# Inverting the pair triangles by 32x32 diagonal blocks in a hybrid DeltaNet and attention decoder step

## What is computed

```python
decay = jnp.where(incl, jnp.exp(jnp.where(incl, diff, 0.0)), 0.0)
L = jnp.where(strict, jnp.einsum('bhnid,bhnjd->bhnij', kb, k) * decay, 0.0)
rhs = jnp.concatenate([vb, kb * jnp.exp(G)[..., None]], axis=-1)
sol = lax.linalg.triangular_solve(L, rhs, left_side=True, lower=True, unit_diagonal=True)
```

## Time and profile before

| | before |
|---|---|
| median of 3 executions (lowest to highest) | 1484.63 us (1483.99 to 1484.95) |
| the profiled execution's own time | 1484.91 us |
| its span in the trace | 1483.1 us |
| TensorE matmuls busy | 1473.2 us (99%), 9284 records |
| VectorE busy | 813.6 us (55%) |
| ScalarE busy | 878.8 us (59%) |
| mean granted TensorE clock | 0.998 |
| DMA | 173.92 MB, mean 117 GB/s |

### The profile page before, as it was taken

The page is one execution under the profiler, slowest core; times in us unless marked ns, Lnnn a source line. Parts: engine busy times, 40 slices in busy tenths (PEclk is TensorE's granted clock), DMA queues, the critical chain, the costliest instruction groups (busy, mean ns, idle before and its releaser), DMA issues.

```text
span 1483.1 us, 26962 instructions
## 1 busy us (share of the span) xinstructions
PE 1473.2 (99%) x9284; PEld 1221.0 (82%) x9284; DVE 813.6 (55%) x1596; ACT 878.8 (59%) x2836; POOL 216.0 (15%) x111
## 2 busy tenths in 40 slices
PE   9999999999999999999999999999999999999998
PEld 7877777877877778778777777788777999999998
DVE  5864445555445563555554555645423766787643
ACT  5545678686566675576855666765766353444432
POOL 3001111211121111111221111111313000000000
PEclk9999999999999999999999999999999999999999
DMA  9542315643245443255323464322654465555551
GB/s 286 169 116 36 78 31 129 153 96 63 61 98 128 119 91 71 61 128 135 83 61 68 102 153 73 68 62 64 169 100 128 151 222 196 171 171 171 190 178 58
DMA packets 263714, 173.92 MB, mean 117 GB/s; under 512 B 165464, under 2 KB 212088, under 8 KB 263448
## 3 DMA queue, kind: packets, MB, share of 16 engines
q1 hardware_dynamic: 263266, 171.94, 44.5%
q10 hardware_dynamic: 318, 0.33, 0.1%
HBM read 132.63 MB, written 6.74 MB: 94 GB/s over the span
## 4 chain that ended last, share of the span: by engine, by line
PE 97%; DVE 2%; ACT 1%; issue 0%; POOL 0%; DVEq 0%; ACTq 0%
PE ps L1991 17%; PE ps L1993 16%; PE ps L1992 16%; PE ps L2400 6%; PE ps L2401 6%; PE ps L2402 5%; PE ps L2031 2%; PE ps L2012 2%; PE ps L2084 2%; PE ps L2348 2%; PE ps L2349 2%; PE ps L2085 2%; PE ps L2086 2%; PE ps L2350 2%; PE ps L1869 2%; PE ps L2150 2%
## 5 line engine op out<-in xcount | busy, mean ns | idle before, releaser
L846 ACT ACTIVATE ksq<-ps 128x128 f32<-128x128 f32 x1024 | 268.1, 276 | 295.0 <-PE ps L1993 293.7
L1991 PE MATMUL ps<-ukh,cTh 128*128 128x512 f32 x1024 | 417.9, 408 | 0.3 <-DVE cTl L1233 0.3
L1993 PE MATMUL ps<-ukh,cTl 128*128 128x512 f32 x1024 | 401.7, 392 | 0.0
L1992 PE MATMUL ps<-ukl,cTh 128*128 128x512 f32 x1024 | 400.4, 391 | 0.0
L700 POOL TENSOR_TENSOR rk<-kss,mhalf 128x32 f32<-128x32 f32 x32 | 179.7, 5616 | 496.8 <-DVE kss L1659 496.8
L1991 PEld LDWEIGHTS ps<-ukh,cTh 128*128 128x128 f32 x1024 | 192.8, 188 | 53.8 <-issue 17.1
L1993 PEld LDWEIGHTS ps<-ukh,cTl 128*128 128x128 f32 x1024 | 192.3, 188 | 42.6
L1992 PEld LDWEIGHTS ps<-ukl,cTh 128*128 128x128 f32 x1024 | 193.2, 189 | 34.1
L846 ACT ACTIVATION_READ_ACCUMULATOR ksq<-ps 128x1 f32 x1024 | 212.2, 207 | 0.0
L834 ACT ACTIVATE cTr<-turned 128x1024 uint16<-128x1024 uint16 x126 | 173.9, 1380 | 10.9 <-PE ps L2015 6.7
L1035 ACT ACTIVATE wh<-wraw 128x2048 fp32r<-128x2048 f32 x44 | 84.3, 1916 | 131.7 <-PE ps L2402 127.2
(11 more groups left out here) (501 smaller groups left out, 2692.4 us busy)
## 6 DMA issues: line engine op xcount, KB each, us to landing
clat<-cache_mla SPq DMA_DIRECT2D x128, 256.0 KB, 2.6
wraw<-w_in SPq DMA_DIRECT2D x16, 1024.0 KB, 5.1
wraw<-w_up SPq DMA_DIRECT2D x16, 1024.0 KB, 5.3
wraw<-w_down SPq DMA_DIRECT2D x16, 1024.0 KB, 5.0
braw<-w_in SPq DMA_DIRECT2D x24, 512.0 KB, 4.1
crope<-cache_mla SPq DMA_DIRECT2D x128, 32.0 KB, 2.4
sst<-state_gdn SPq DMA_DIRECT2D x32, 128.0 KB, 3.3
gdn_sample<-sst SPq DMA_DIRECT2D x32, 128.0 KB, 2.0
```

The costliest lines, as they stand in the source:

```text
L846: i = nc.scalar.activation(ksq[:, P * h:P * h + P], ps[:, k % 3, P * h:P * h + P], ACT.Square, accum_out=kss[:, n // 4 % 2, n % 4, 4 * hal ...
L1991: mm(out, cTh[:, n % 2, c], ukh[:, c, cols], start=c == 0, stop=False)
L1992: mm(out, cTh[:, n % 2, c], ukl[:, c, cols], start=False, stop=False)
L1993: i = mm(out, cTl[:, n % 2, c], ukh[:, c, cols], start=False, stop=c == 3)
```

## The change

The diagonal blocks of 32x32 are inverted apart, in compact tiles Tc, Uc and Xc of 128x(4x32): partition block q holds the q-th diagonal block of each of the four triangles. Levels 1 to 4 are products of 32x32x32, one for each block and triangle (16 for x, 16 for t), each on its own rows and columns of the array. VectorE makes the transpose Uc from Tc itself, by an instruction that turns each 32x32 block (5 for each pair), instead of TensorE (L2141, L2154) and ScalarE (L957). At k = 30 VectorE spreads Tc and Uc into T_ (now 128x(4x64)) and U_ (zeroed first). Level 5 is done on blocks of 32 (8 products at k = 30, 12 at k = 31) and level 6 on blocks of 64 (4 products at k = 32, 4 at k = 33). The masks of the constants shrink from 128 to 32 columns (`consts` loses 800 columns, 410 KB of one DMA). The cut places are marked by "...".

```diff
--- before.py
+++ after.py
@@ -62,14 +62,15 @@
 C_ID, C_BD, C_ROT, C_ONE = _col(P), _col(P), _col(P), _col(P)
 C_COS, C_SIN = _col(T), _col(T)
 C_INCL, C_STRICT = _col(P), _col(P)
-C_LVL = [_col(P) for _ in range(LEVELS)]
+C_LVL = [_col(32) for _ in range(5)]
 C_NEG = _col(3 * P)
 C_ZW = _col(48)
 C_ZP = _col(16)
 C_RSC = _col(1)
 C_RIN = _col(1)
 C_RSQ = _col(1)
-C_LVT = _col(P)
+C_LVT = _col(32)
+C_IDC = _col(32)
 C_THIRDS = _col(16)
 C_HEADS = _col(8)
 C_ALL = _at
@@ -90,19 +91,20 @@
     c[:, C_SIN] = np.tile(np.sin(ang).T, (4, 1))
     c[:, C_INCL] = k <= m
     c[:, C_STRICT] = k < m
+    r, m32 = k % 32, np.arange(32)[None, :]
     for s, at in enumerate(C_LVL):
         b = 1 << s
-        c[:, at] = (k // (2 * b) == m // (2 * b)) & (k % (2 * b) >= b) & (m % (2 * b) < b)
+        c[:, at] = (r // (2 * b) == m32 // (2 * b)) & (r % (2 * b) >= b) & (m32 % (2 * b) < b)
     neg = np.where(m > k, np.float32(-1e30), np.float32(0.0))
     c[:, C_NEG] = np.concatenate([neg, np.zeros((P, P)), neg], 1)
     c[:, C_ZW.start + 15] = 1
     c[0:64, C_ZP.start + 6] = c[64:128, C_ZP.start + 7] = 1
...
-    c[:, C_LVT] = c[:, C_LVL[0]].T
+    c[:, C_LVT] = (r == m32 - 1) & (r % 2 == 0)
+    c[:, C_IDC] = r == m32
     c[:, C_HEADS] = k % 32 == m[:, 0:8]
     c[0:96, C_THIRDS] = k[0:96] % 32 == m[:, 0:16]
     return c
@@ -134,11 +136,11 @@
 F_END = F_ATT + H + 3
 STEPS = list(range(14)) + [None, 14, 15, 16, None] + list(range(17, 47))
 B_START, B_SLOTS = F_END + 6, len(STEPS)
-PAIR_A = ([f"p{j}" for j in range(6)] + ["gr0", "gr1", "l2r", "br0", "br1", "lb0", "lb1", "lb2", "lb3", "qk", "kk", "qks", "kqs", "x0", "kqsT", "x1", "t1"])
+PAIR_A = ([f"p{j}" for j in range(6)] + ["gr0", "gr1", "l2r", "br0", "br1", "lb0", "lb1", "lb2", "lb3", "qk", "kk", "qks", "kqs", "kqsT", "x1", "t1"])
 for _s in range(2, LEVELS):
     PAIR_A += [f"x{_s}", f"t{_s}" if _s < LEVELS - 1 else f"u{_s}"]
 PAIR_A += ["uu0", "out0", "o0", "s0", "ks", "out1", "uu1", "o1", "s1", "out2", "out3", "osr", "ob0", "ob1"]
-PAIR_B = ["cs", "rwA", "rwB", "vt", "kt", "ut1", "krow", "ut2", "urow", "ut3", "ut4", "ut5"]
+PAIR_B = ["cs", "rwA", "rwB", "vt", "kt", "krow", "urow"]
 FRONT_A = ["ns", "rots", "qrow0", "qrow1", "rope0", "rope1", "qcol0", "qcol1", "rope2", "rope3", "rot0", "rot1", "rot2", "rot3", "snew"]
 FRONT_A += [f"nope{h % 2 * H + h // 2}" for h in range(2 * H)]
 for _j in range(H + 3):
@@ -367,9 +369,12 @@
         tail, e = place("tail", [P, 6, 11], F32, e)
         assert e <= TOP, e
         gw, e = place("gw", [64, 5, T], F32, EARLY)
-        T_, e = place("T_", [P, 4, CH], F32, EARLY)
+        T_, e = place("T_", [P, 4, 64], F32, EARLY)
+        Tc, e = place("Tc", [P, 4, 32], F32, e)
+        Uc, e = place("Uc", [P, 4, 32], F32, e)
         U_, e = place("U_", [P, 4, CH], F32, e)
         X_, e = place("X_", [P, 4, CH], F32, e)
+        Xc, _ = place("Xc", [P, 4, 32], F32, taken["X_"][0])
         rhs_, _ = place("rhs_", [P, 2, CH], F32, taken["X_"][0])
         osq, _ = place("osq", [P, 2, T], F32, EARLY)
         uu, e = place("uu", [P, 2, CH], F32, e)
@@ -953,8 +958,6 @@
                     for w in range(4):
                         i = nc.scalar.activation(kd[:, w, :], bank[:, CH * w:CH * w + CH], ACT.Copy, scale=colb[:, 1, w % 2, w // 2:w // 2 + 1])
                     i.then_inc(S("b_read"), 1)
-                if 24 <= k < 34 and k % 2 == 0:
-                    nc.scalar.activation(U_[:].rearrange("p u n -> p (u n)"), rows_out(f"ut{(k - 22) // 2}_{b}"), ACT.Copy).then_inc(S("b_read"), 1)
                 if k == 25:
                     bank = rows_out(f"krow_{b}")
                     nc.scalar.activation(kst[:], bank[0:96, 0:P], ACT.Copy)
@@ -1439,10 +1442,13 @@
             def four(ap):
                 return ap.rearrange("p (u n) -> p u n", n=CH)
 
-            idb = consts[:, C_ID].unsqueeze(1).to_broadcast([P, 4, CH])
+            idc = consts[:, C_IDC].unsqueeze(1).to_broadcast([P, 4, 32])
+
+            def blocks(ap):
+                return ap.rearrange("p (u n) -> p u n", n=32)
 
             def level_mask(cols_):
-                return consts[:, cols_].unsqueeze(1).to_broadcast([P, 4, CH])
+                return consts[:, cols_].unsqueeze(1).to_broadcast([P, 4, cols_.stop - cols_.start])
 
             def pair_dve(b, k):
                 def bank(name):
@@ -1502,8 +1508,12 @@
                     V.tensor_tensor(small(2), sample_of(0), sample_of(2), ALU.mult).then_inc(S("sample_ready"), 1)
                 if k == 20:
                     v.wait_ge(S("a_read"), a_count(f"kk_{b}"))
-                    link(V.tensor_tensor(U_[:], lT[:], level_mask(C_LVT), ALU.mult))
-                    V.tensor_tensor(U_[:], idb, U_[:], ALU.subtract).then_inc(S("tri_start"), 1)
+                    for q in range(4):
+                        r = slice(32 * q, 32 * q + 32)
+                        i = V.tensor_tensor(Uc[r], lT[r, :, r], level_mask(C_LVT)[r], ALU.mult)
+                    link(i)
+                    link(V.tensor_tensor(Uc[:], idc, Uc[:], ALU.subtract))
+                    V.transpose(Tc[:].rearrange("p u n -> p (u n)"), Uc[:].rearrange("p u n -> p (u n)")).then_inc(S("tri_start"), 1)
                     v.wait_ge(S("decay_exp"), 3 * b + 3)
                     V.tensor_tensor(qkv[:, 0:2, 0:TP], qkv[:, 0:2, 0:TP], eg[:, :, 0:TP], ALU.mult).then_inc(S("qg_scaled"), 1)
                     V.tensor_copy(sm[:, 6], bank("qks")[:, 0:2 * NS]).then_inc(S("a_read"), 1)
@@ -1517,20 +1527,35 @@
                 if k == 28:
                     v.wait_ge(S("b_read"), b_count(f"urow_{b}"))
                     V.tensor_tensor(ust[64:96], kraw[64:96], ust[64:96].bitcast(F32), ALU.subtract).then_inc(S("ust_ready"), 1)
-                if k == 21:
-                    V.tensor_tensor(T_[:], four(bank("x0")), level_mask(C_LVL[0]), ALU.mult).then_inc(S("a_read"), 1)
-                    v.wait_ge(S("a_read"), a_count(f"x0_{b}"))
-                    V.tensor_tensor(T_[:], idb, T_[:], ALU.subtract).then_inc(S("tri_start"), 1)
-                if 22 <= k < 34 and k % 2 == 0:
+                if 22 <= k < 30 and k % 2 == 0:
                     s_ = (k - 22) // 2 + 1
-                    V.tensor_tensor(X_[:], four(bank(f"x{s_}")), level_mask(C_LVL[s_]), ALU.mult).then_inc(S("a_read"), 1)
-                if 22 <= k < 34 and k % 2 == 1:
+                    V.tensor_tensor(Xc[:], blocks(bank(f"x{s_}")[:, 0:128]), level_mask(C_LVL[s_]), ALU.mult).then_inc(S("a_read"), 1)
+                if 22 <= k < 30 and k % 2 == 1:
                     s_ = (k - 22) // 2 + 1
-                    if s_ < LEVELS - 1:
-                        V.tensor_tensor(T_[:], T_[:], four(bank(f"t{s_}")), ALU.subtract).then_inc(S("a_read"), 1)
-                    else:
-                        v.wait_ge(S("b_read"), b_count(f"ut{s_ - 1}_{b}"))
-                        V.tensor_tensor(U_[:], U_[:], four(bank(f"u{s_}")), ALU.subtract).then_inc(S("a_read"), 1)
+                    V.tensor_tensor(Tc[:], Tc[:], blocks(bank(f"t{s_}")[:, 0:128]), ALU.subtract).then_inc(S("a_read"), 1)
+                    v.wait_ge(S("a_read"), a_count(f"t{s_}_{b}"))
+                    V.transpose(Uc[:].rearrange("p u n -> p (u n)"), Tc[:].rearrange("p u n -> p (u n)")).then_inc(S("tri_start"), 1)
+                if k == 30:
+                    p_ = blocks(bank("x5")[:, 0:128])
+                    V.tensor_copy(Xc[32:64], p_[32:64])
+                    V.tensor_copy(Xc[96:128], p_[96:128]).then_inc(S("a_read"), 1)
+                    V.memset(T_[0:32], 0.0)
+                    link(V.memset(U_[:], 0.0))
+                    v.wait_ge(S("tri_start"), 5 * b + 5)
+                    for q in range(4):
+                        r = slice(32 * q, 32 * q + 32)
+                        V.tensor_copy(U_[r, :, r], Uc[r])
+                        if q < 2:
+                            V.tensor_copy(T_[r, :, r], Tc[r])
+                if k == 31:
+                    p_ = bank("t5")
+                    V.tensor_scalar(T_[32:64, :, 0:32], blocks(p_[32:64, 0:128]), -1.0, None, ALU.mult)
+                    V.tensor_scalar(U_[0:32, :, 32:64], blocks(p_[0:32, 128:256]), -1.0, None, ALU.mult)
+                    V.tensor_scalar(U_[64:96, :, 96:128], blocks(p_[64:96, 128:256]), -1.0, None, ALU.mult).then_inc(S("a_read"), 1)
+                if k == 32:
+                    V.tensor_copy(X_[64:128, :, 0:64], bank("x6")[64:128, 0:256].rearrange("p (u n) -> p u n", n=64)).then_inc(S("a_read"), 1)
+                if k == 33:
+                    V.tensor_scalar(U_[0:64, :, 64:128], bank("u6")[0:64, 0:256].rearrange("p (u n) -> p u n", n=64), -1.0, None, ALU.mult).then_inc(S("a_read"), 1)
                 if k == 21:
                     bank("kqsT")
                     at_ = B_PAIR + SIDE_A.index(f"kqsT_{b}") % 2
@@ -2138,30 +2163,58 @@
                     a_done(i)
                 if k == 21:
                     read("kk")
```

(72 more changed lines are left out.)

## The result

The changed kernel takes 1457.26 us, median of 4 runs (1456.79 to 1457.93), against 1484.31 us for the kernel before (1483.70 to 1484.95): ratio 0.9819, 95% interval 0.9808 to 0.9831, 27 us less. The forecast was 1462 us and 22.7 us less. Two later sets of the unaltered kernel gave 1458.97 (1456.98 to 1459.30) and 1457.52 us (1457.00 to 1459.06), 0.9825 and 0.9823 of the kernel before.

A forecast was written before the change was run, and what follows sets the result against it. TensorE was taken to bound the kernel: 13.5 us a pair falls away and 7.8 comes, 5.7 less, 22.7 us in all, from 1484.9 to 1462.2, so 1462 us. The range ran from 1456, with one to spare, to 1478.

The forecast's parts named there:

- What bounds: Whole kernel: TensorE, busy 99% of the span, so a microsecond off its queue is a microsecond of the kernel.
- What falls away: TensorE's old full-array products and transposes in the inverse: 13.5 us a pair, 54 us in four pairs.
- What comes: TensorE's new small products in the inverse: 8.4 us a pair, 7.8 after slots following query products or weighing.
- The fixed part: Each slot of the inverse on TensorE: leaving the full array and coming back costs 0.34 us.
- the saving behind a tiled visit: Three of twelve slots follow query products or weighing, full array already left: 0.13 instead of 0.34 us, 0.2 less each.
- I take 42 ns, the middle: Time of a pass of four small products on TensorE, between bounds of 27 and 56 ns; a slot 0.68 us.
- VectorE: Its masking, subtraction, turning and copies in the inverse grow at some steps but stay covered: cost nothing.
- The cover at k = 30 to 32: VectorE's 5.3 us of work fits into TensorE's 6.1 us before k = 32, with 0.8 us to spare.
- rival 2: VectorE late at k = 30 to 32, small operations costing twice: 3 us a pair, 1474; chance with mixtures 0.10.
- Rival 1: Small products on TensorE don't run side by side: 1481 to 1515 us; chance 0.07 if perfectly pipelined, 0.11 at 56 ns.
- rival 1a: Small products one after another, perfectly pipelined, 27 to 33 ns a record: about no change, 1481 to 1487; chance 0.07.
- Start: Shorter constants, 410 KB less in one DMA needed late: 0, at most 1 us gained at the start.

The follow-up runs named there:

- b_noturn: The kernel before without the 20 sets of four TensorE transposes of T_ and the ScalarE copies to U_; 1476.18 us, 0.9945 of the kernel before.
- a_dve1: The changed kernel with two more clearings of U_ on VectorE at k = 30; 1458.83 us in one run.
- a_dve4: The changed kernel with eight more clearings of U_ on VectorE at k = 30; 1478.75 us, 0.9956 of the kernel before.
- a_serial: The changed kernel with all 16 products of a slot of levels 1 to 4 on block 0, blocks 1 to 3 left out; 1481.43 us, 0.9981.
- a_twice: The changed kernel with every product of levels 1 to 4 issued twice; 1468.26 us, 0.9892 of the kernel before.
- a_powers: The changed kernel with 32x32 blocks inverted by powers of N, five slots instead of eight a pair; 1455.35 us, 0.9802 of the kernel before.
- a_order: The changed kernel with loops exchanged in levels 1 to 4, all four triangles of one block before the next block; 1471.32 us, 0.9912.

## Why the prediction came out as it did

- **What bounds.** Right. What went from TensorE's queue went from the time: 26.9 us in the slots of the inverse, 27.0 between the first and the last key product, 27 in the medians.
- **What falls away, 13.5 us a pair.** Right where it could be tested: b_noturn has the 0.45 us of four transposes and the 0.90 of four products. Its sum of 9.0 us came out as 8.7 in the slots, of which 8.2 reached the distance of the key products and 7.9 the median. Counted in every slot of the trace before, less what the work beside it costs where it stands alone, 13.4 us a pair fell away.
- **What comes, 8.4 us before sharing, 7.8 a pair.** This is the term that was mis-sized: counted in the same way, 6.8 us a pair came, 1.0 less. That 13.5 - 27.0 / 4 = 6.75 gives the same is partly luck, for two small things that the sum did not have cancel: 0.1 us a pair less fell away, and 0.1 us a pair was gained where a transpose for another step (L2166, L2169 before; L2219, L2222 now) stands behind a product of the inverse in one slot and adds 0.05 us instead of 0.11. The fixed part was right: 0.34 taken, 0.58 - 8 x 0.031 = 0.33 found; so was the saving behind a tiled visit (0.2), and k = 32 (0.80 taken and found). The step that failed is "I take 42 ns, the middle": a pass took 31 ns. Ten slots of eight passes at 11 ns less are 0.9 of that 1.0 us a pair. The row that had made the upper bound, 56 ns for a 24x24 transpose, loads 128 columns of weights each time, as I had said beside it and then not used: nothing else spoke for the upper half.
- **VectorE.** Right, and its prices too: turning 0.31 us (0.3 taken), clearing 0.485 (0.48), copies inside SBUF 0.22 (0.28 taken). The cover at k = 30 to 32, forecast as 0.8 us to spare, was 1.4 us at its thinnest, held for the 1.3 us more of a_dve1 and broke under a_dve4. Had rival 2 come true, its price of 3 us a pair would have been too low, for it left out the clock.
- **Rival 1.** What decides is whether four products run side by side, and the equality was set at 31 ns a record: a_serial has 31 ns a record and lands 0.2% from the kernel before, most of which is k = 30 and 31. (The lower end of rival 1a should have read 1480: 27 ns gives 4.4 us less by the prediction's own formula.) The Trainium skill's rule (TensorEngine Tiling (Array Packing), Gotcha 1) that different row tiles cannot access one PSUM bank at the same time would put the four products of a pass in a row, and that is not what was measured: four row groups write one bank, four records start within 0.04 us, and a pass of four takes 31 ns, as long as one record alone in a_serial. The measurement decides. How the writes into the bank follow each other inside these 31 ns no trace shows.
- **Start.** 0 to 1 us for the shorter constants was not seen apart: the first key product started 0.6 us earlier in one profile of the changed kernel and 0.9 later in the other.

## What to carry over

On a kernel bound by TensorE, small work beside a stream of full products has two prices: leaving the full array and coming back, here 0.33 us however much is done there, and passes of 0.031 us if neighbours in program order sit on different row and column groups. So cut problems into 32x32 blocks, put the loop over blocks innermost, and then gather as many independent products as there are into one visit, next to other tiled work where that stands. Price an idle gap of TensorE with the clock in it, not by its length alone.

## What the runs showed of the chip

- One part of the array takes a 32-column float32 record every 31 to 32 ns (a_serial), though the slope over columns gives 27 ns. Parts beside each other don't slow each other: 16, 24 or 32 records of eight passes all cost 0.57 to 0.58 us in a slot (k = 30, 31 and 22).
- In a slot of 64 records the second 32 cost 0.30 us where the first, beyond the fixed part, cost 0.25 (a_twice; the same 0.88 us in a_powers). The starts lose their rhythm of four after some 34 records and come in twos from there, about 17 ns apart. What sets that pace wasn't tested.
- A row group that follows another in program order is begun before the first is done, also when each has eight records (a_order: 22 ns a record).
- A wait of 3.8 us cost 6.2, one of 3.6 cost 5.3, and two of 2.1 cost 3.7 and 5.1: the rest is key products at the lower granted clock, at 0.43 us instead of 0.23, for some 5 us behind the wait in pair 0 (a_dve4).
